# Probabilities times values with the values stationary: two heads side by side in the array, rows divided by their sums on GpSimd before they are turned

## The reference

```
def mla_attend(q_nope, q_rope, k_nope, k_rope, v, mask):
    s = (jnp.einsum('bqhd,bkhd->bhqk', q_nope, k_nope, preferred_element_type=jnp.float32)
         + jnp.einsum('bqhr,bkr->bhqk', q_rope, k_rope, preferred_element_type=jnp.float32)) * ATTN_SCALE
    if mask is not None:
        s = jnp.where(mask, s, NEG_INF)
    p = jax.nn.softmax(s, axis=-1).astype(v.dtype)
    return jnp.einsum('bhqk,bkhd->bqhd', p, v)
```

## Time and profile before

| | us |
|---|---|
| median of 3 runs (lowest, highest) | 1511.6 (1511.08, 1513.78) |
| profiled execution, its own time | 1514.12 |
| its span, first to last instruction | 1512.3 |
| mean granted TensorE clock | 0.995 of 2.4 GHz |
| PE busy in the span | 1485.5 (98%) |
| DVE / ACT / GpSimd busy | 805.0 / 618.8 / 697.0 |

### The profile page before, as it was taken

The page is one execution under the profiler, slowest core; times in us unless marked ns, Lnnn a source line. Parts: engine busy times, 40 slices in busy tenths (PEclk is TensorE's granted clock), DMA queues, the critical chain, the costliest instruction groups (busy, mean ns, idle before and its releaser), DMA issues.

```text
span 1512.3 us, 29016 instructions
## 1 busy us (share of the span) xinstructions
PE 1485.5 (98%) x10592; PEld 1406.6 (93%) x10592; DVE 805.0 (53%) x1397; ACT 618.8 (41%) x1236; POOL 697.0 (46%) x453
## 2 busy tenths in 40 slices
PE   9999999999999999999999999999999999999998
PEld 7789999999999999998987878787999999999998
DVE  6005716755645636547856464556456636456365
ACT  4413201123534434335448475656225434344342
POOL 7454454453363543634766061514243544635434
PEclk9999999999999999999999999999999999999999
DMA  7322232222132231321532010101122231412312
GB/s 231 89 82 82 67 111 83 62 77 70 57 128 69 84 101 48 128 84 55 163 112 74 2 56 1 55 0 55 42 70 57 84 118 50 137 57 83 111 55 90
DMA packets 36384, 120.32 MB, mean 80 GB/s; under 512 B 6040, under 2 KB 6744, under 8 KB 36064
## 3 DMA queue, kind: packets, MB, share of 16 engines
q1 hardware_dynamic: 30240, 109.20, 23.5%
q10 hardware_dynamic: 6080, 10.28, 2.2%
HBM read 115.91 MB, written 3.55 MB: 79 GB/s over the span
## 4 chain that ended last, share of the span: by engine, by line
PE 48%; ACT 2%; DVE 2%; issue 1%; ACTq 0%; DVEq 0%
PE ps L649 8%; PE ps L651 8%; PE ps L650 8%; PE ps L785 5%; PE ps L787 5%; PE ps L786 5%; PE ps L1040 2%; PE ps L1019 2%; PE ps L975 1%; PE ps L989 1%; PE ps L1048 1%; ACT kT L1894 1%; PE ps L978 1%; DVE neg_max L1541 1%; PE ps L954 1%
## 5 line engine op out<-in xcount | busy, mean ns | idle before, releaser
L649 PE MATMUL ps<-h_hi,w_hi 128*128 128x288 f32 x1280 | 380.6, 297 | 0.0
L650 PE MATMUL ps<-h_lo,w_hi 128*128 128x288 f32 x1280 | 377.5, 295 | 0.0
L651 PE MATMUL ps<-h_hi,w_lo 128*128 128x288 f32 x1280 | 376.3, 294 | 0.0
L590 POOL TENSOR_TENSOR w_lo<-raw,w_hi 128x512 fp32r<-128x512 f32 x128 | 173.5, 1365 | 220.7 <-ACT w_hi L1722 220.5
L785 PE MATMUL ps<-op_hi,w_hi 128*128 128x288 f32 x896 | 266.4, 297 | 4.4 <-DVE x L1338 4.3
L786 PE MATMUL ps<-op_lo,w_hi 128*128 128x288 f32 x896 | 265.0, 296 | 0.0
L787 PE MATMUL ps<-op_hi,w_lo 128*128 128x288 f32 x896 | 264.1, 295 | 0.0
L651 PEld LDWEIGHTS ps<-h_hi,w_lo 128*128 128x128 f32 x1280 | 241.1, 188 | 0.0
L649 PEld LDWEIGHTS ps<-h_hi,w_hi 128*128 128x128 f32 x1280 | 239.8, 187 | 1.2
L650 PEld LDWEIGHTS ps<-h_lo,w_hi 128*128 128x128 f32 x1280 | 240.3, 188 | 0.0
L581 POOL TENSOR_TENSOR w_lo<-raw,w_hi 128x1024 fp32r<-128x1024 f32 x60 | 145.2, 2425 | 183.9 <-ACT w_hi L1714 183.9
(11 more groups left out here) (200 smaller groups left out, 2755.5 us busy)
## 6 DMA issues: line engine op xcount, KB each, us to landing
raw<-stream SPq DMA_DIRECT2D x206, 512.0 KB, 3.6
out_x<-x ACTq DMA_DIRECT2D x8, 288.0 KB, 2.5
x<-xt SPq DMA_DIRECT2D x4, 288.0 KB, 5.9
x<-xt ACTq DMA_DIRECT2D x4, 288.0 KB, 9.1
raw<-stream ACTq DMA_DIRECT2D x2, 512.0 KB, 7.0
b_bc<-bs ACTq DMA_DIRECT2D x2, 512.0 KB, 6.6
cache_raw<-cache_ct ACTq DMA_DIRECT2D x1, 1024.0 KB, 5.5
v_out<-sgu_grow ACTq DMA_DIRECT2D x1, 512.0 KB, 4.9
```

Of the source, the lines that this page charges most:

```text
L590: nc.gpsimd.tensor_tensor(block_of(w_lo, b), factor(i, b), block_of(w_hi, b).bitcast(F32), ALU.subtract).then_inc(split_lo, 1)
L649: nc.tensor.matmul(out, l_hi, r_hi, start=first, stop=False)
L650: nc.tensor.matmul(out, l_hi, r_lo, start=False, stop=False)
L651: return nc.tensor.matmul(out, l_lo, r_hi, start=False, stop=last)
```

## The change

For a prompt item the roles in the product with the values are exchanged: the values of a head (64 columns) are stationary and 128 turned probabilities move. The result is already feature-major (64 features by 128 queries), the two heads of a pair go to partitions 0 to 63 and 64 to 127 of one bank, and their matmuls alternate, so one `pv` step now takes a piece of each head. Since queries now lie along the free axis, the division by the row sums can't be done on the output: it is done on the probabilities before they are turned. For each item DVE inverts its sums (`invert_sum`, 18 a group instead of 6), GpSimd multiplies the item's row with them (18 a group, new), and PE's `turn` waits for GpSimd (`scaled`).

The transposes of the gather, `o_tok` and its multiplications are gone. ACT and DVE split the output straight from its bank (`high_out`, `low_out`, four parts a group). Items now go by pairs of heads, `(0,0) (1,0) (0,1) (1,1) ...`; `probs` and `turned` have four buffers instead of three. The last `pv` of a group (pair 1, block 3) is done behind the first unit of the next group's queries, and in group 3 inside the first tile of the o projection.

```diff
-PROMPT = [("prompt", h, b) for h in range(HG) for b in range(4)]
+PROMPT = [("prompt", 2 * a + hh, b) for a in range(HG // 2) for b in range(4) for hh in range(2)]
...
+                for n, (kind, a, blk) in enumerate(ITEMS):
+                    at = stat_of(n)
+                    pool.reg_mov(units, g * NI + (n + 1))
+                    pool.wait_ge(set_up, SETUPS)
+                    pool.wait_ge(inv_sums_set, units)
+                    row = (probs[:, PROMPT.index(ITEMS[n]) % DEEP, 0:(blk + 1) * P] if kind == "prompt"
+                           else probs_s[:, a, :])
+                    nc.gpsimd.tensor_scalar(row, row, inv_sums[:, at:at + 1], None, ALU.mult).then_inc(scaled, 1)
...
+            def times_values(n, g):
+
+                kind, a, blk, pieces = PV[n]
+                waited = {("prompt", 1, 0): 1, ("prompt", 1, 1): 2}.get((kind, a, blk))
+                for p in pieces:
+                    pe.reg_mov(filled, g * pieces_by(p) + (p // 2 + 1))
+                    pe.wait_ge(ident_set, 1)
+                    pe.wait_ge(piece_set(p), filled)
...
+                for m, kt in enumerate(PIECES[pieces[0]][1]):
+                    for hh in range(2):
+                        h = 2 * a + hh
+                        to = slice(hh * VD, hh * VD + VD)
+                        if kind == "prompt":
+                            bank = SAMPLE_OUT if (a, blk) == (1, 0) else PROMPT_OUT
+                            at = P if (a, blk) == (1, 0) else blk * P
+                            last = nc.tensor.matmul(ps[to, bank, at:at + P], vals[:, kt, h * VD:(h + 1) * VD],
+                                                    turned[:, pieces[hh] % DEEP, m * P:(m + 1) * P],
+                                                    start=(kt == 0), stop=(kt == blk), skip_group_check=True)
...
+                        elif k == 0 and t == 1 and not first:
+                            pe.wait_ge(piece_odd, g * (NP - EVEN_PIECES))
...
-                        else:
-                            gather(1, g - 1)
+                    elif k == 0 and not first:
+                        times_values(NV - 1, g - 1)
...
+                    if p < RING:
+                        pe.reg_mov(filled, g * NI + (SAMPLE_ITEM + (1 if p < 2 else 2)))
+                        pe.wait_ge(ident_set, 1)
+                        pe.wait_ge(probs_set, filled)
+                    pe.reg_mov(filled, g * NI + (item + 1))
...
-                    pe.wait_ge(probs_set, filled)
+                    pe.wait_ge(scaled, filled)
...
-                            last = nc.tensor.matmul(ps[:, out_bank(o), blk * VD:(blk + 1) * VD],
-                                                    turned[:, p % RING, n * P:(n + 1) * P],
-                                                    vals[:, kt, a * VD:(a + 1) * VD],
-                                                    start=(kt == 0), stop=(kt == blk))
...
-            pe.wait_ge(hid_ready, B_O + 7)
+            pe.wait_ge(piece_odd, NG * (NP - EVEN_PIECES))
+            pe.wait_ge(out_read, NO * NG - 2)
             o_parts(range(0, 2))
-            gather(1, NG - 1)
+            times_values(NV - 1, NG - 1)
...
+            def low_out(n, g):
+
+                kt = g * 2 + n // 2
+                dve.wait_ge(out_hi, g * NO + (n + 1))
+                for src, lo, hi in out_part(n):
+                    last = nc.vector.tensor_tensor(hid_lo[:, ds(kt, 1), lo:hi], src.unsqueeze(1),
+                                                   hid_hi[:, ds(kt, 1), lo:hi].bitcast(F32), ALU.subtract)
+                last.then_inc(out_read, 1)
...
+                def invert_sum(i):
+                    at = stat_of(i)
+                    dve.wait_ge(probs_set, g * NI + (i + 1))
+                    nc.vector.reciprocal(inv_sums[:, at:at + 1], sums[:, at:at + 1]).then_inc(inv_sums_set, 1)
...
                         row_max(SAMPLE_ITEM, sample_scores(0))
-                        dve.wait_ge(probs_set, g * NI + (SAMPLE_ITEM + 1))
+                        for i in range(SAMPLE_ITEM + 1):
+                            invert_sum(i)
                         row_max(SAMPLE_ITEM + 1, sample_scores(1))
...
+                    if step == "score" and inverted:
+                        while inverted < n:
+                            invert_sum(inverted)
+                            inverted += 1
```

More of the change, by code:

```diff
@@ L137, in attention_order @@
             steps += [("fill", first_ahead[-1]), ("score", first_ahead[-1])]
-        ahead = 4 * a + blk + 3
-        if kind == "prompt" and 2 * RING <= ahead < len(PROMPT):
-            steps.append(("score", ITEMS.index(PROMPT[ahead])))
+        if kind == "prompt":
+            ahead = PROMPT.index(ITEMS[item]) + RING
+            if 2 * RING <= ahead < len(PROMPT):
+                steps.append(("score", ITEMS.index(PROMPT[ahead])))
         steps.append(("turn", p))
[L142 to L147, removed]
+        steps += [("out", n) for n in outs]
+        outs = []
+        if p == PV[pv_of(p)][3][-1]:
+            owed.append(pv_of(p))
+        while owed and PV[owed[0]][3][-1] <= p - 2:
+            v = owed.pop(0)
+            steps.append(("pv", v))
+            if PV[v][:3] in OUT_AFTER:
+                outs.append(OUT_AFTER[PV[v][:3]])
+    for v in owed[:-1]:
+        steps.append(("pv", v))
+        if PV[v][:3] in OUT_AFTER:
+            outs.append(OUT_AFTER[PV[v][:3]])
+    return steps + [("out", n) for n in outs]
 ORDER = attention_order()
@@ L173, in score_banks @@
     for step in ORDER:
-        if step[0] == "score" or step == ("gather", 0):
-            n = 1 if step[0] == "score" else 2
+        if step[0] == "score":
+            n = 1
             banks = [SCORE_BANK + (at + i) % RING for i in range(n)]
@@ L474, in latent_bank, with out_part @@
             return 2 + L % 3 if L < NT else 5 + (L - NT) % 3
[L476 to L482, removed]
+        def out_part(n):
+            bank = ps[:, PROMPT_OUT, :]
+            side = ps[:, SAMPLE_OUT, :]
+            if n == 0:
+                return [(side[:, 0:DEC], SEQ, T)]
+            if n == 1:
+                return [(bank, 0, SEQ)]
+            if n == 2:
+                return [(side[:, 0:DEC], SEQ, T), (side[:, P:2 * P], 0, P)]
+            return [(bank[:, P:SEQ], P, SEQ)]
         def latent_target(L):
@@ L922, in head_group @@
                         pe.wait_ge(q_read, g * NT + NT)
-                    elif j and not first:
-                        pe.wait_ge(hid_ready, g * 2 + B_O)
+                    elif not first:
+                        pe.wait_ge(out_read, g * NO)
                     for k in range(2):
@@ L1942, in head_group @@
                         take_piece(act, nc.scalar.copy, n, g, piece_even)
-                    elif step == "gather":
-                        gather(n, g)
+                    elif step == "out":
+                        high_out(n, g)
             head_group(0, True)
@@ L1948, in _ @@
                 head_group(g, False)
-            gather(1, NG - 1)
+            high_out(NO - 1, NG - 1)
+            act.sem_inc(hid_hi_set, 2 * NG)
             operands(3, F_O)
```

191 lines of the change are left out of this document (66 added, 125 removed).

## The result

The changed kernel takes 1528.41 us (median of 4 runs, 1527.67 to 1528.60), the kernel before, beside it on the same chip, 1511.47 us (4 runs, 1511.08 to 1513.78): a ratio of 1.010, 95% interval 1.0083 to 1.0117, so slower by 13 to 18 us. The forecast was 1496.5 us, range 1489 to 1505, with 0.06 for slower.

The account below looks back on a forecast made before the run. PE, busy 98% of the span, was taken as the bound. Per group -2.2 - 1.6 - 0.6 + 0.7 = -3.7 us, x4 plus 0.45 = -14.4: 1497.2 from the 1511.6 median, forecast 1496.5 with rounding, range 1489 to 1505.

Parts of the forecast that it names:

- term 4: Start of each head group: PE's wait for the second sample's exponentials, then for item (1,1)'s division on GpSimd; +0.7 us a group.
- later items: Items behind a group's start: PE's own work covers reciprocal and division, so nothing charged; 0.3 us to spare at the tightest.
- GpSimd is slower than its nearest row: Rival: at 2.37 us for 1024 columns, divisions at a group's start end 1.7 us later a group; 1503 us, chance 10%.
- The clock falls oftener: Rival: PE's clock, seen falling in one of four group starts, falls in two more; 1503 us, 8% for more falls.
- the forecast's sum: -3.7 us a group, times four -14.8, plus 0.45 once at the o projection: -14.4 us for the whole kernel.
- Term 1: PE's product of prompt items with the values: 6.0 us against 8.2, switches of stationary width included; -2.2 us a group.
- The rule of the Trainium skill: Rival in the prompt product: stationary loads overlap matmuls only across different row groups, so loads not hidden; 1505 us, chance 8%.
- serial heads: Rival in the prompt product: a pair's two heads run one after the other, 4.4 us a group; 1514 us, chance 3%.
- Term 2: The two gathers of five transposes each on PE, about 0.75 us each, go away; -1.6 us a group.
- term 3: PE's waits for `o_tok`, outputs that DVE has not taken, go away; -0.6 us a group.
- Term 5: Group's last product, moved into the next group's queries: copy wait covered there; about 0.45 us wait once, at the o projection.
- The rival that ended slower: Rival: divisions late at every item, about 13 items 0.4 to 0.5 us late, 5.5 us a group; 1518 us, chance 5%.

Follow-up runs that it names:

- the last experiment: Changed kernel with GpSimd's two-tensor product, the second sample item divided later, and 5 identity matmuls (8 in the run before) ahead of the samples' scores: 1498.77 us, ratio 0.9904.

## Why the prediction was wrong

**The step that failed is the price of GpSimd's division in term 4**, "1088 columns at 1.04 us for 1024", used again under "later items". The row was TENSOR_SCALAR, the right name, but L566's scalars are constants; the change's scalar is read from memory. Measured: 3.04 us instead of 1.15. The same name hid another operand form, and the experiment with constants, which has no wait at any turn, shows that the rest of the step would have held at the price assumed.

**The same step took GpSimd to be idle when the second sample's reciprocal comes.** At these prices it is not. In group 1 three prompt blocks end at 903.48 and the first sample item about 906.5; the second ends at 909.51. The second sample's reciprocal is there at 905.37, when the first sample item still has 1.15 us to go. With GpSimd 2.6 times as dear, the queue, and not the last reciprocal, sets the turn's time. That is why the rival "GpSimd is slower than its nearest row" was too small as well. It had the right mechanism and place, but took 2.37 us for 1024 columns, and counted only what the second item and (1,1) add, 1.7 us a group; the wait is 3.1 to 3.55. And it stopped at 1503 because it counted nothing behind the wait.

**What the wait does to the clock was not connected with it.** "The clock falls oftener" stood as a rival of its own at 8%, as if it were chance. It is tied to the first step: the wait of 3.1 to 3.55 us at the fourth turn had the low clock behind it in all four groups (1.2 of 2.4 GHz, for 23.9 us in all by windows of 0.2 us, so 12 us lost), and with matmuls in the wait in none. The rest of the 18.6, some 7 us, was lost in the samples' scores of three groups, against 3.3 in one group before; that part may be chance, since in the other kernels without a filler there one to three groups had it.

The balance, in us of the span: the forecast's sum -14.4; waits at the fourth turn 13.8, less the 0.8 that term 4 allowed, +13.0; the wait of 0.25 near each group's end, +1.0; the clock, 18.6 less 3.3, +15.3. Together +14.9, and the spans differ by 14.4. That it closes within 0.5 us is partly luck: inside the -14.4 two terms are wrong in opposite directions, as follows.

Point by point, the other terms:

- **Term 1, the product: right in kind, worth half of what was said.** An L904 of 16 records takes 1.02 us from start to start (0.9 to 1.0 forecast), of 12 0.81, of 4 0.37. What was missed is a fixed 0.15 us in each of the 8 steps (0.37 for 4 records costed at 0.22, 1.02 for 16 at 0.88), on top of the 0.1 ahead and behind. So the term is near -1.0 a group instead of -2.2. The fixed part could have been read in the earlier trace rows: at 0.11 us for two records of 128 columns side by side, the samples' 12 records of 64 columns would be 0.33 us, and the row says 0.49; the prediction took the whole as 0.04 a record. It also counted 32 records for a block that has 16 (4 tiles, 2 heads, 2 passes); the length it gave was for 16. The halves do overlap with 128 moving columns, with the loads hidden: 12 more records are 0.65 us, 0.054 each. The rule of the Trainium skill (TensorE: Matmul & The Clock Gate, The mechanism) that spoke against it does not hold in these rows, nor do serial heads.
- **Term 2, the gathers, and term 3, the waits for `o_tok`:** both are gone. They were not tested apart.
- **Term 4 without the price:** in the version without the division no turn waits, not even the third, which waited 0.3 us before. So the 0.7 is too much. What is seen of it is that PE, with less work ahead of the samples' scores, waits 0.3 us longer there for `kT`: 0.77 and 0.93 us, against 0.54 and 0.87 in group 1 before.
- **Term 5:** the moved product takes 1.02 us in the next group's queries, and PE waits 0.42 us once for the copy ahead of the o projection, against 0.45.
- **The sum:** from group 1's first score to group 2's it was 69.9 us before and is 66.5 in the last experiment (883.47 to 950.00): -3.4, against -3.7 forecast. Term 1's miss of 1.2 is half made up by term 4, where +0.3 stands for +0.7 and a wait of 0.3 is gone; the hit of the sum is thus no evidence for its terms.
- **The rival that ended slower** had another mechanism, divisions late at every item. From "above 3 ns a column" it was to decide; at 2.56 the later items were nearly covered, as the single 0.25 us wait shows. The loss came at one place, where two long items stood ahead of a short one, on an engine that had been idle until then.

What stays open: why the clock falls behind the samples' wait in some groups and not in others, of the same kernel. The fillers show that the idle ahead of it is needed; what picks the group no run here shows.

## What to carry to other kernels

A row prices an instruction only if its operand form is the same too: for a scalar, see whether the row's operands name a tensor for it or not, and look through all rows of the engine for one with the same operands. When work moves to an engine that was idle, add up its queue in order up to the first item that somebody waits for, and ask whether a long item that is needed late stands ahead of a short one that is needed now; an order changed by one item was worth some 20 us here (1.010 to 0.9965). And where PE is the bound, cost a wait of PE twice: its length, and the clock behind it.

## What the runs showed of the hardware

- GpSimd, 1088 columns in and out in float32: 1.10 us with constants, 2.00 as a product of two tensors (one repeated along the row), 3.04 with a scalar from memory; DVE does the last in 0.79. The Trainium skill, GPSIMD Engine Reference, section 4.1 (Engine selection), calls operations with one input roughly line-rate, and section 3.1 has a higher cost only for two inputs. The form with constants agrees; the one with a scalar from memory does not, and is dearer than the product of two tensors.
- DVE's product with a scalar, from and to SBUF, took 1.15 and 1.17 us instead of 0.35 and 0.42 when GpSimd multiplied at the same time, and ended before GpSimd did in the first case; GpSimd, and DVE's copy from PSUM, took no longer.
- A wait of 3.1 to 3.55 us had the clock at its lower level behind it every time in the changed kernel, one of 1.0 to 1.2 us in one group of four; 0.8 and 0.9 us one after the other ahead of the samples' scores sometimes did. Five small matmuls in the second of them kept it up in all four groups.
